# Hybrid encoder block: a head's back half two steps behind its front half, keys transposed by DMA

## The reference

```python
proj = h @ w_in                       # 1024 -> 8 x 1024: q, f, i, gate, glu value, glu gate, gate a, gate b
f = lb + (1 - lb) * sigmoid(f_logit); k = 1 - f; g = log(f); q = silu(q_in) * 128 ** -0.5
# per head (8 heads, 128 x 128 state), in chunks of 64 frames:
#   S_t = diag(f_t) S_(t-1) + k_t^T v_t ;  o_t = S_t^T q_t
y_a = (rms_norm(o) * silu(o_gate)) @ w_hg_out
u = glu_v * sigmoid(glu_g)
y_b = silu(layer_norm(causal_depthwise_conv(u, 31 taps))) @ w_conv_out
h = layer_norm(alpha * h + (sigmoid(gate_a) * y_a + sigmoid(gate_b) * y_b) @ w_out)
h = layer_norm(alpha * h + (silu(ffn_g) * ffn_u) @ w_ffn_out)       # hidden size 2816
```

## Time and profile before

| | |
|---|---|
| median of 3 runs | 2373.98 us (2373.38 to 2491.91) |
| profiled execution, its own time | 2374.15 us |
| its span on the slowest core | 2372.6 us (all cores: 2363.0 to 2372.6) |
| granted TensorE clock, mean of the span | 0.993 of full speed |
| busy share of the span | PE 96%, DVE 55%, ACT 49%, POOL 21% |
| chain that ended last | PE 84%, DVE 5%, ACT 5%, issue 4%, DMA 2% |

### The profile page before, as it was taken

How to read it: one execution, slowest core, us unless ns; L and a number is a source line. 1 busy time by engine, 2 the same in 40 slices (tenths; PEclk the granted TensorE clock), 3 DMA queues, 4 the chain that set the end, 5 groups by cost and what they waited for, 6 DMA issues and landing times.

```text
span 2372.6 us, 39997 instructions; the slowest of 8 cores (2363.0 to 2372.6 us)
## 1 busy us (share of the span) xinstructions
PE 2282.4 (96%) x13569; PEld 1149.2 (48%) x13838; DVE 1298.2 (55%) x1919; ACT 1170.2 (49%) x1678; POOL 504.0 (21%) x599
## 2 busy tenths in 40 slices
PE   7999999999999789999999999999999999999998
PEld 3555555555555543444444444444444444444443
DVE  3666665666667774555553643636444545454434
ACT  4777777878888784444442422323223232322220
POOL 4444344444344253333320000000000000000000
PEclk9999999999999999999999999999999999999999
DMA  9555362653541437253335343645444343535340
GB/s 160 96 112 99 66 125 40 116 108 55 109 85 54 130 83 161 72 117 99 90 80 158 125 149 107 173 130 156 137 148 142 120 156 109 159 103 167 88 152 36
DMA packets 125542, 270.88 MB, mean 114 GB/s; under 512 B 39488, under 2 KB 64192, under 8 KB 121792
## 3 DMA queue, kind: packets, MB, share of 16 engines
q1 hardware_dynamic: 106576, 203.03, 27.2%
q0 software_dynamic: 18768, 65.28, 17.5%
HBM read 275.88 MB, written 61.87 MB: 142 GB/s over the span
## 4 chain that ended last, share of the span: by engine, by line
PE 84%; DVE 5%; ACT 5%; issue 4%; DMA 2%; POOL 1%; DVEq 0%; ACTq 0%; another core or an unknown queue 0%; SPq 0%; POOLq 0%
PE psb L421 83%; ACT L442 1%; DMA sb_y<-yD 1%; DVE sb_YT L490 1%; ACT sb_F L442 1%; DVE sb_Tb L474 1%; PE psb L426 1%; DMA sb_W<-w 1%; ACT sb_rso L442 1%; DVE sb_y L474 0%; DVE sb_ub L474 0%; ACT sb_U L442 0%; DVE sb_F L639 0%; DVE sb_y L450 0%; DVE sb_Qp L450 0%
## 5 line engine op out<-in xcount | busy, mean ns | idle before, releaser
L421 PE MATMUL psb<-sb_xT,sb_W 128*128 128x512 bf16 x2437 | 711.1, 384 | 19.8 <-DMA sb_xT<-xt 5.8
L421 PE MATMUL psb<-sb_hT,sb_f1r 128*128 128x512 bf16 x2760 | 687.1, 379 | 3.2
L442 ACT ACT_TABLE_LOAD x283 | 363.1, 1283 | 434.7 <-PE psb L421 261.9
L421 PEld LDWEIGHTS psb<-sb_hT,sb_f1r 128*128 128x128 bf16 x2816 | 275.5, 98 | 332.2
L421 PE MATMUL psb<-sb_W,sb_xT 128*128 128x128 bf16 x2048 | 404.2, 221 | 12.2 <-DVE sb_vt L481 4.1
L421 PE MATMUL psb<-sb_wf,sb_actb 128*128 128x512 bf16 x1381 | 338.0, 379 | 1.5 <-DVE sb_actb L450 0.2
L421 PEld LDWEIGHTS psb<-sb_xT,sb_W 128*128 128x128 bf16 x2560 | 240.1, 99 | 186.9 <-issue 36.4
L421 PE MATMUL psb<-sb_xT,sb_wj 128*128 128x512 bf16 x995 | 305.6, 379 | 3.4 <-ACT sb_hT L442 1.3
L450 DVE TENSOR_TENSOR sb_actb<-sb_sg,psb 128x512 bf16<-128x512 f32 x176 | 118.1, 684 | 245.8 <-PE psb L421 154.2
L442 ACT ACTIVATE sb_sg<-psb 128x512 f32<-128x512 f32 x176 | 101.9, 596 | 291.0 <-PE psb L421 273.4
L421 PEld LDWEIGHTS psb<-sb_W,sb_xT 128*128 128x128 bf16 x2048 | 195.2, 99 | 69.8 <-issue 13.7
(11 more groups left out here) (105 smaller groups left out, 2747.4 us busy)
## 6 DMA issues: line engine op xcount, KB each, us to landing
sb_f1r<-f1D SPq DMA_DIRECT2D x176, 512.0 KB, 4.3
sb_Tp<-tp POOLq DMA_DIRECT2D x32, 512.0 KB, 8.5
yD<-sb_YT SPq DMA_DIRECT2D x32, 512.0 KB, 9.0
sb_y<-yD SPq DMA_DIRECT2D x64, 256.0 KB, 3.4
sb_R<-x SPq DMA_DIRECT2D x32, 512.0 KB, 5.5
out<-sb_R SPq DMA_DIRECT2D x32, 512.0 KB, 2.8
sb_W<-w POOLq DMA_DIRECT2D x47, 256.0 KB, 5.4
f1D<-wf POOLq DMA_DIRECT2D x22, 512.0 KB, 6.1
```

Source lines behind the costliest of these rows:

```text
L421: return P.add("pe", lambda e: e.matmul(o, lhsT=l, rhs=r, start=start, stop=stop), ks(lhsT, rhs), out.k, dur=max(60, fsz(r)) / 2400.0 + 0. ...
L442: return P.add("act", lambda e: e.activation(out=o, in_=i, func=func, **kw), rd, out.k, dur=0.19 + fsz(o) / 1200.0 + 0.09 * ptr, tbl=ACT_S ...
```

## The change

Step s of the loop now runs `back(s - 1)`, `front(s + 1)` and the same `glu` and `conv`; step 0 has no back, and in the last step `back(62)` is followed by `back(63)`. What a front hands on has three buffers (Qp, Qx, Kb, og, vt, Kt, Eb, chosen by s % 3); K2 keeps two, F, Tb, Am and oo too; osq and rso have one instead of two. The four TensorE transposes of K2 and ACT's copy into Kt leave `back`; `front` ends with one DMA transpose of K2 (128x512) straight into Kt, issued from SP, with one semaphore for each of K2's two buffers.

```diff
-        Qp = [b(f"Qp{p}", [4, 128], BF16) for p in range(2)]
+        Qp = [b(f"Qp{p}", [4, 128], BF16) for p in range(3)]
...
-        Kt = [b(f"Kt{p}", [4, 128], BF16) for p in range(2)]
+        Kt = [b(f"Kt{p}", [4, 128], BF16) for p in range(3)]
...
-        osq = [b(f"osq{p}", [TS], BF16) for p in range(2)]
-        rso = [b(f"rso{p}", [TS], F32) for p in range(2)]
+        osq = [b("osq0", [TS], BF16)] * 2
+        rso = [b("rso0", [TS], F32)] * 2
...
         def front(s):
             h, t = divmod(s, 8)
             p = s % 2
+            r = s % 3
...
             tt(K2[p].all(), kv[:, 64:192], e2.bc(2, [128, 4, 128]), ALU.mult, eng="pool")
+            dmatr(Kt[r].all(), K2[p].all().r("p b q -> p (b q)"), f"kt{p}")
             yield
...
         def back(s):
             h, t = divmod(s, 8)
             p = s % 2
-            ps = newps()
-            psv = V(psb[ps][:].bitcast(BF16), [("ps", ps)])
-            for bb in range(4):
-                tr(V(psv.ap[:, bb * 128:bb * 128 + 128], psv.k), K2[p][bb, :])
-            cp(Kt[p].all(), V(psv.ap[:, 0:512].rearrange("p (a b) -> p a b", a=4), psv.k), eng="act")
-            relps(ps)
-            yield
+            r = s % 3
...
-                mm(pv(psK, bb * 128, bb * 128 + 128), Kt[p][bb, :], vt[p][bb, :], True, True)
+                mm(pv(psK, bb * 128, bb * 128 + 128), Kt[r][bb, :], vt[r][bb, :], True, True)
...
-            gens = [back(s)]
+            gens = [back(s - 1)] if s > 0 else []
             if s + 1 < 64:
                 gens.append(front(s + 1))
...
+            if s == 63:
+                gens[0] = chain(gens[0], back(63))
             run(gens)
```

More of the change, by code:

```diff
@@ L354, in build_nc @@
         F = [[b(f"F{i}_{p}", [TS], F32) for i in range(4)] for p in range(2)]
-        Qp = [b(f"Qp{p}", [4, 128], BF16) for p in range(2)]
-        Qx = [b(f"Qx{p}", [4, 64], BF16) for p in range(2)]
-        Kb = [b(f"Kb{p}", [4, 192], BF16) for p in range(2)]
+        Qp = [b(f"Qp{p}", [4, 128], BF16) for p in range(3)]
+        Qx = [b(f"Qx{p}", [4, 64], BF16) for p in range(3)]
+        Kb = [b(f"Kb{p}", [4, 192], BF16) for p in range(3)]
         K2 = [b(f"Kc{p}", [4, 128], BF16) for p in range(2)]
-        og = [b(f"og{p}", [TS], BF16) for p in range(2)]
-        vt = [b(f"vt{p}", [4, 128], BF16) for p in range(2)]
-        Kt = [b(f"Kt{p}", [4, 128], BF16) for p in range(2)]
+        og = [b(f"og{p}", [TS], BF16) for p in range(3)]
+        vt = [b(f"vt{p}", [4, 128], BF16) for p in range(3)]
+        Kt = [b(f"Kt{p}", [4, 128], BF16) for p in range(3)]
         Tb = [b(f"Tb{p}", [4, 128], BF16) for p in range(2)]
-        Eb = [b(f"Eb{p}", [4], F32) for p in range(2)]
+        Eb = [b(f"Eb{p}", [4], F32) for p in range(3)]
         Am = [b(f"Am{p}", [4, 128], BF16) for p in range(2)]
-        osq = [b(f"osq{p}", [TS], BF16) for p in range(2)]
-        rso = [b(f"rso{p}", [TS], F32) for p in range(2)]
+        osq = [b("osq0", [TS], BF16)] * 2
+        rso = [b("rso0", [TS], F32)] * 2
         oo = [b(f"oo{p}", [TS], F32) for p in range(2)]
@@ L624, in front @@
             F0, F1, F2, F3 = F[p]
-            for (w, dst, fn) in ((wf, F1, AF.Tanh), (wq, F0, AF.Silu), (wo, og[p], AF.Silu)):
+            for (w, dst, fn) in ((wf, F1, AF.Tanh), (wq, F0, AF.Silu), (wo, og[r], AF.Silu)):
                 ps = newps()
@@ L648, in front @@
                     yield
-            cp(vt[p].all(), pv3(ps, 4))
+            cp(vt[r].all(), pv3(ps, 4))
             relps(ps)
@@ L655, in front @@
             e2 = V(f2v.ap[:, :, 127], F1.all().k)
-            tt(Qp[p].all(), V(F0.h[:].rearrange("p (b q) -> p b q", b=4), F0.all().k), f2v, ALU.mult)
-            tt(Eb[p].all(), e1, e2, ALU.mult, eng="pool")
-            tt(Qx[p].all(), Qp[p][:, 64:128], e1.bc(2, [128, 4, 64]), ALU.mult)
+            tt(Qp[r].all(), V(F0.h[:].rearrange("p (b q) -> p b q", b=4), F0.all().k), f2v, ALU.mult)
+            tt(Eb[r].all(), e1, e2, ALU.mult, eng="pool")
+            tt(Qx[r].all(), Qp[r][:, 64:128], e1.bc(2, [128, 4, 64]), ALU.mult)
             act(F2.all(), F2.all(), AF.Exp, scale=-1.0)
             yield
-            kv = Kb[p]
+            kv = Kb[r]
             kout = V(kv.h[:].rearrange("p b (s q) -> p b s q", s=3)[:, :, 0:3:2, :], kv.all().k)
@@ L683, in back @@
                     c0 = bb * 128 + hf * 64
-                    mm(pv(psA, c0, c0 + 64), Kb[p][bb, hf * 64:hf * 64 + 128], Qp[p][bb, hf * 64:hf * 64 + 64], True, True)
+                    mm(pv(psA, c0, c0 + 64), Kb[r][bb, hf * 64:hf * 64 + 128], Qp[r][bb, hf * 64:hf * 64 + 64], True, True)
             tt(Am[p].all(), pv3(psA, 4), mask.bc(1, [128, 4, 128]), ALU.mult)
@@ L697, in back @@
                 dst = Tb[p][bb + 1, :] if bb < 3 else Tb[1 - p][0, :]
-                stt(dst, Tb[p][bb, :], Eb[p][bb:bb + 1], pv(psK, bb * 128, bb * 128 + 128), ALU.mult, ALU.add)
+                stt(dst, Tb[p][bb, :], Eb[r][bb:bb + 1], pv(psK, bb * 128, bb * 128 + 128), ALU.mult, ALU.add)
                 if bb % 2 == 1:
@@ L705, in back @@
                 c0 = bb * 128
-                mm(pv(psO, c0, c0 + 128), vt[p][bb, :], Am[p][bb, :], True, False)
-                mm(pv(psO, c0, c0 + 64), Tb[p][bb, :], Qp[p][bb, 0:64], False, False)
-                mm(pv(psO, c0 + 64, c0 + 128), Tb[p][bb, :], Qx[p][bb, :], False, True)
+                mm(pv(psO, c0, c0 + 128), vt[r][bb, :], Am[p][bb, :], True, False)
+                mm(pv(psO, c0, c0 + 64), Tb[p][bb, :], Qp[r][bb, 0:64], False, False)
+                mm(pv(psO, c0 + 64, c0 + 128), Tb[p][bb, :], Qx[r][bb, :], False, True)
             sq = act(osq[p].all(), pv(psO), AF.Square)
-            stt(oo[p].all(), pv(psO), gn, og[p].all(), ALU.mult, ALU.mult, after=[sq])
+            stt(oo[p].all(), pv(psO), gn, og[r].all(), ALU.mult, ALU.mult, after=[sq])
             relps(psO)
```

## The result

The changed kernel takes 2400.19 us in the median of 4 runs (2397.88 to 2401.92), the kernel before 2375.77: a ratio of 1.0105, with a 95% interval of 1.0092 to 1.0118. The forecast was 2333 us, the range 2304 to 2376: the time is 67 us over the forecast and outside the range. In some executions of these kernels two neighbouring cores, or a whole die, are granted a lower clock for 160 us or longer and end later by it (2491.91 us is one of the four times of the kernel before): the ratios leave the slowest of such executions out, the medians do not, and where it matters the time without it is given. The spans of the cores are 2389.5 to 2400.4 us; the page is of core 3.

The account below looks back on a forecast made before the run. PE, busy 96% of the 2372.6 us span, was taken as the bound. Removed work 14.1, handover 20 and last steps 7 made 41 us off 2374.15, so 2333 us, range 2304 to 2376.

Parts of the forecast that it names:

- The removed work: All 64 steps: 256 transpose matmuls off PE at 0.055 us each, 14.1 us gained (0 to 19).
- The handover: 50 to 750 us: two-step handover removes most PE waits for vt, Qp, Am, Tb and two half-clock stretches, 20 us (0 to 29).
- B: Rival: only the removed work pays, the new order has as many waits as the old; 2360 us, chance 0.20.
- The price of the DMA transpose: Each step's Kt: landing 4.0 us after issue, some 3.4 us later than before, hidden by a median room of 11.5 us.
- Rival C: Transposes queued behind yD or onD stores land late, PE stands, 8.6 us each; 2402 to 2471 us, chance 0.08.
- The last steps: 750 to 950 us, steps 55 to 63: longer handover gains, shrinking room may show latency; 7 us gained (-26 to +34).

Follow-up runs that it names:

- the three pairs: At planner latency 0.38, 0.40, 0.42: kernel before 2386.8, 2374.0, 2400.6; two-step handover, PE transposes 2355.3, 2360.6, 2369.6; same with DMA after step 2 2374.1, 2362.7, 2393.9 us.
- the handover alone: The changed kernel with all 64 transposes on PE at the end of the front half, copied by ACT, no DMA transpose in the loop: 2360.6 us, ratio 0.9948.
- at 0.40: The planner's latency between engines (XLAT) at its usual 0.40 us: kernel before 2374.0, two-step handover with PE transposes 2360.6, changed kernel 2400.2 us.
- the change at 0.42: The changed kernel with the planner's latency between engines at 0.42 instead of 0.40 us: 2458.5 us, some 2415 without the lower clock on two cores.
- the plain copy: The changed kernel with each DMA transpose replaced by a plain DMA copy of the same 128 KB, transposition left out: 2392.6 us, measured once.

## Why the prediction was wrong

Of the 41 us forecast as gained 16 came, from 200 to 700 us, and 1 was lost again behind them; the 43 us lost before 200 us stood nowhere in the sum.

**The removed work** (14.1 us): it is there. Between 200 and 700 us, some 36 steps by 500 us over about 14 us each, the DMA transposes made 73 more weight loads than PE transposes with the same handover: 13 us, against 36 x 4 x 0.055 = 8 us of slots. But over the whole kernel the DMA transposes gave no time back in any of the three pairs. By the 390 ns of the Trainium skill (VectorE: DVE Perf Modes, section The three transpose paths) the same 144 transposes would have been an estimated 56 us; the trace doesn't bear that out.

**The handover** (20 us): the sign holds, the reason only half. The waits for vt and Qp went as said. But from 200 to 700 us the list of PE's waits is as long as before, 16.1 us against 17.6, with rso, oo and U in place of vt, Qp and Am; in this one pair B had the list right. Of the 16 us regained there 13 are the removed transposes and 1 the handover. Over three pairs of orders the handover alone is worth 25 us in the mean, near the 20 that were taken. It gives them in other places than was said: at 0.40 mostly after 700 us. What I had not asked is how far an order packed anew moves by itself: 27 us for the kernel before, more than the term. The prediction's 2% as the least that can be told is not the limit, for 1.0105 has an interval of 1.0092 to 1.0118; the packing is.

**The price of the DMA transpose** is the step that failed. I took 4.0 us from the earlier trace rows, rows of a stage in which DMA was busy 45% of the time, for 64 transposes of which the first two stand in a stretch where it is busy 99%. In quiet stretches a landing is 2.3 us, better than taken; beside the input's load it is 30.2. (By the prediction's own numbers Kt comes 4.0 - 0.22 - 0.59 = 3.2 us later, not 3.4, which changes nothing.) And I set it against the median room of 11.5 us, although the smallest, 0.06 us, stands at step 0 in both orders: the order itself showed that the first step has no long handover. The two together make the 28.8 us wait. The planner, too, took a fixed landing and so put nothing behind it: told of the loads in flight, it left one wait of 2.2 us.

**Rival C** had the mechanism, transposes that land late behind other traffic, and its price of one: a stall and a slow clock behind it. It had the place wrong. Beside yD's stores landings did reach 19.3 us, yet that cost one wait of 4.0 us and one of 2.1, since the room there was real. It put 0.08 on a case that took place, and did not name the stretch that the first DMA slices of the page before, 9 and then 5, should have made me look at first:

```profile
DMA  9555362653541437253335343645444343535340
```

**The last steps** (7 us): net 1 us lost after 700 us instead. One wait for Kt, 2.0 us, was there, and Am's 6.1 us and a new one of 3.2 for cbf came in where vt's went from 4.6 to 2.3. The handover with all transposes on PE did gain some 10 us there, so it is the DMA transposes, or the order packed around them, that took it back; which, no run shows.

## What to carry to other kernels

A small latency-bound transfer pays in packets, not in bytes: look at the DMA share of the very stretch in which it is issued, above all at the start of a program, and take the shortest room there, not the median. Where a planner packs the order, run the old kernel with one of its constants nudged before believing any difference of a per cent; several pairs tell a design from a packing. And look at the granted clock of every core before explaining 20 or 30 us of the slowest one. A longer handover was the good half of this change, and alone it beats both kernels.

## What the runs showed of the hardware

A DMA transpose of 128x512 two-byte values is 544 packets, a plain copy of the same bytes 144, and on full DMA engines one or two packets of the other queue went by for each of them (674 for 543, 874 for 544, 1188 for 544; 273 for the copy's 144), so that the landing follows the other's packet size: 30.2 us beside packets of 7.3 KB in the mean, 15.3 beside 2.9 KB, 13.2 beside 1.8 KB, 2.3 with the other queues quiet. That they take turns is inferred from these counts; the views do not show which packet waited for which. The Trainium skill (Advanced Engine Details and Errata, section X-Bar Transpose (TRN2)) says that transpose DMAs are as fast as regular ones; in quiet stretches the two land in 2.3 and 1.9 us, which is near it, and beside the input's load in 30.2 and 11.9, which does not agree.

Beside the two levels of the granted clock there is 0.81, in stretches of 160 us on two neighbouring cores (0 and 1 of the change at 0.42, 6 and 7 of the plain copy): 1087 matmuls in 160 us in place of 1313.
